# Triangular inverses of the recurrent mixer on 32x32 diagonal blocks: 48 small products in four diagonal array tiles and one eviction per step

## Chip, cores and metric

The kernel runs on one core of one Trainium2 chip (trn2). The metric is the device time of one execution in microseconds (us). Everything is float32; the large projections are made of two or three float32r passes over a high and a low part of each operand.

## What is computed

The reference is two transformer blocks over 256 tokens of width 1024. The first block's mixer has three parts, of which one is a recurrent mixer with six heads of 64 channels. This is the only part that the change touches:

```python
def step(S, inp):
    r_t, d_t, k_t, v_t, kk_t, a_t = inp
    sa = jnp.einsum('bhij,bhj->bhi', S, -kk_t)
    S = S * d_t[:, :, None, :] + sa[..., None] * (kk_t * a_t)[:, :, None, :] + v_t[..., None] * k_t[:, :, None, :]
    return S, jnp.einsum('bhij,bhj->bhi', S, r_t)

_, o = lax.scan(step, S0, tuple(tm(t) for t in (r_h, d_h, k_h, v_h, kk, a_h)))
```

The kernel does not scan token by token. It takes 32 tokens at a time: inside such a chunk the correction `sa` is the solution of a triangular system, whose matrix is unit-triangular and 32x32, so it needs the inverse (I - N)^-1 of eight chunks for each of six heads. The chunks are then joined by a state that is carried from one to the next.

## The kernel before, in words

One program for the core, written engine by engine: a block for TensorE (`pe`), VectorE (`dve`), ScalarE (`act_`), GpSimd (`pool`) and the DMA queue of SyncE. Order on each engine is the order of the code; semaphores join them. PSUM has eight banks; `opened(job)` takes the next bank in rotation and waits until its last reader gave it back, `close` signals `psum_ready`, a reader calls `take(job)` and its last instruction gives the bank back (`freed(job)`), and `copied(job)` lets TensorE wait for that.

All matmuls are issued from one helper, `mm` (line 572 before, 570 after), and transposes from lines 582 (`turn`), 1037 and others, so rows are told apart by operand names, shapes and time. A float32 product of this helper stands in the trace as two MATMUL records, each with a LDWEIGHTS record of its own; a transpose as one.

The work around the change, in the order of TensorE:

- Attention rounds of the second mixer part, with one `ada()` group after each. A group is 8 products of streamed weights (128 rows, 32 columns, 512 moving columns), in four column tiles of the array. Its weights come through a ring of six 1 MB slots.
- `gram("N", s)` and `gram("L", s)` for the two halves `s` of the tokens: 24 products of 64 rows, a 128x128 result per half and head. Heads stand as three pairs `c` with two members `p`; each (s, p) has a bank, with three 128-column results.
- VectorE multiplies those results with masks that leave 8x8 blocks of the 32x32 diagonal blocks (`U8`, `L8M`), and signals `tri_first`.
- The inverse: 11 steps, listed in `INV` (L2, N2, L4, Y1, T8, T8t, Ya, T16, T16t, Yb, T32), from 8x8 blocks by doubling to 32x32. A step is done for the four (s, p) in turn: three 128x128x128 products (or three transposes, in T8t and T16t), one bank, one eviction. Of steps that only copy, VectorE evicts p = 0 and ScalarE p = 1; of steps that add, VectorE evicts all four. The matrices are 128x128 with zeros outside the 32x32 diagonal blocks. After Y1 and after Ya stand two groups of three transposes (`tokens_out`), after T8 and T16 an `ada()` group, after Yb the gram MT of half 0.
- After T32: grams Rb and Rk of half 0, an `ada()` group, `masked_values(0)` (mv), `solved(0)` (au: the inverse times its right-hand sides, 12 products for both p in pairs of 128 columns), `blocks(0)`, and the chain over states; half 1 follows. On VectorE, after T32's evictions come six masked evictions of MT, Rb, Rk, five `low_part` of the first projection's input, and then the eviction of mv.
- The four matrices of a step lie in `TM[s][i]`, `KEEP[s][3]` holds the finished inverse. GpSimd builds the masks once, in its set-up before 31 us, ahead of the tables for the third mixer part (the S5 scan), whose last signal is `tables`.

Of the kernel before, what the change touches and what calls it, by code (L numbers as in the profile page):

```python
# [10 lines left out]
F32 = mybir.dt.float32  # L11
# [5 lines left out]
P = 128  # L17
# [56 lines left out]
def two_block_kernel(nc, a, out):  # L74
    ctx = ExitStack()
    with ctx:
# [42 lines left out]
        cond = sb("cond", KT)  # L119
        first_gain = sb("first_gain", KT)  # L120
# [33 lines left out]
        def parts(name, off, *dims):  # L154
# [54 lines left out]
        TM = [[at(M0 + 768 * i, 2, 3, P) for i in range(6)] + [at(M0 + 15360 + 768 * i, 2, 3, P) for i in range(3)],  # L209
              [at(o, 2, 3, P) for o in (2816, 3584, 4352, 5664, 6432, M0 + 17664, M0 + 18432)] +  # L210
              [place("hn_a", HN, F32, 2, 3, P), place("hn_b", HN + KT * T, F32, 2, 3, P)]]
        KEEP = [[at(M0 + 12288 + 768 * i, 2, 3, P) for i in range(4)],
                [TM[0][4], TM[0][5], TM[1][7], at(768, 2, 3, P)]]
# [271 lines left out]
        def tmat(s, i):  # L485
            return KEEP[s][3] if i == 9 else TM[s][i]

        @block.tensor
        def _(pe):
# [77 lines left out]
            def copied(job):  # L567

                pe.wait_ge(*freed(job))
# [440 lines left out]
            def gram(name, s):  # L1010
                lw, rw = {"N": (7, 6), "L": (6, 7), "MT": (8, 6), "Rb": (7, 9), "Rk": (8, 9)}[name]
# [42 lines left out]
            def solved(s):  # L1054
                copied(("mv", s))
                for p in range(2):
                    copied(("T32", s, p))
# [68 lines left out]
            for s in range(2):  # L1126
                for p in range(2):
                    copied(("N", s, p))
# [452 lines left out]
        def _(pool):  # L1581
# [44 lines left out]
            led.emit(g.tensor_tensor(L16M, L16M, L8M, ALU.subtract))  # L1626
            keep_if(row_ok[:, :], ALU.is_ge, -31, 1, [[P, 2]])
# [132 lines left out]
        def _(dve):  # L1760
# [429 lines left out]
            for s in range(2):  # L2190
                for p in range(2):
                    b = take(("N", s, p))
                    tt(TM[s][0][:, p], three(b), over3(U8), MUL, *freed(("N", s, p)))
                for p in range(2):
                    b = take(("L", s, p))
                    tt(TM[s][1][:, p], three(b), over3(L8M), MUL, sem("tri_first"))
            settle()
            for s in range(2):
                for p in range(2):
# [942 lines left out]
```

## Time and profile before

| | |
|---|---|
| three timed runs | 1310.95 us median (1309.79 to 1317.23) |
| the profiled execution | 1307.66 us, of it 1305.9 us span |
| granted TensorE clock, mean | 0.983 of 2.4 GHz |
| PE (TensorE matmul) busy | 1254.2 us, 96% of the span |
| PEld (its weight loads) busy | 1119.7 us, 86% |
| DVE (VectorE) busy | 601.3 us, 46% |
| ACT (ScalarE) busy | 653.2 us, 50% |
| POOL (GpSimd) busy | 846.8 us, 65% |
| HBM traffic | 240.11 MB read, 1.05 MB written |

Times in rows are microseconds from the span's start. "Idle before" is how long the engine stood still ahead of a row, and the arrow names what ended that. A matmul's end is modelled by the profiler, its start is recorded; busy time is the union of records, so overlapping matmuls count once, and (x96) counts records. Several records of one kind in a row are merged into one line with their count.

### The profile page before, as it was taken

The page shows a single profiled execution, that of the slowest core. Times are in us where ns is not written, and L with a number is a line of the kernel's source. Part 1 is how long each engine was busy: PE and PEld are TensorE (multiplying, and loading weights), DVE is VectorE, ACT ScalarE, POOL GpSimd, SP SyncE. Part 2 cuts the span into 40 slices and gives each one's busy share as a digit, 9 for nine tenths or more (in the row PEclk, how much of TensorE's full clock was granted, in tenths as well). Part 3 has the DMA queues.
Part 4 walks back from the last instruction along what each step waited for, and adds up shares of the span by engine and source line. Part 5 has one row for each costly group of instructions (what it writes and reads, how often), then busy time and mean ns, then how long its engine had stood idle before and what let it go on. Part 6 is the DMA issues. An engine that isn't in the chain of part 4 may idle for free.

```text
span 1305.9 us, 24860 instructions
## 1 busy us (share of the span) xinstructions
PE 1254.2 (96%) x10093; PEld 1119.7 (86%) x10093; DVE 601.3 (46%) x1369; ACT 653.2 (50%) x1074; POOL 846.8 (65%) x445
## 2 busy tenths in 40 slices
PE   6997988889999999999999999999999999999998
PEld 6993547679899999999988889998988789988887
DVE  6658687642676695432555512412111114555411
ACT  5531343125755554654666643656554554655642
POOL 8984500025788877664788777667765655888782
PEclk8998999989999999999999999999999999999999
DMA  8859895603465555435555566443648893455550
GB/s 263 214 169 376 316 343 209 212 29 102 158 194 177 171 178 186 162 129 162 161 191 183 175 194 194 130 147 113 194 134 262 266 294 120 160 189 193 178 177 33
DMA packets 232943, 242.76 MB, mean 186 GB/s; under 512 B 9196, under 2 KB 201854, under 8 KB 232830
## 3 DMA queue, kind: packets, MB, share of 16 engines
q1 hardware_dynamic: 232510, 241.08, 57.0%
q8 instruction: 80, 1.31, 0.4%
q14 instruction: 33, 0.27, 0.1%
q10 hardware_dynamic: 320, 0.10, 0.0%
HBM read 240.11 MB, written 1.05 MB: 185 GB/s over the span
## 4 chain that ended last, share of the span: by engine, by line
PE 80%; DVE 5%; ACT 2%; issue 1%; POOL 1%; DMA 0%; DVEq 0%; SPq 0%; ACTq 0%
PE banks L572 79%; DVE arena L1804 1%; DVE banks L1804 1%; DVE arena L1797 1%; PE banks L1428 1%; ACT ring_hi L2569 1%; POOL ring_lo L1716 1%; ACT arena L2569 1%; DVE hn_lo L1804 1%; DMA ring<-in_w_kv_dram 0%; DVE banks L1797 0%; DVE arena L1810 0%; PE banks L582 0%; PE banks L914 0%; PE banks L1037 0%
## 5 line engine op out<-in xcount | busy, mean ns | idle before, releaser
L1716 POOL TENSOR_TENSOR ring_lo<-ring,ring_hi 128x2048 fp32r<-128x2048 f32 (+1 forms) x176 | 717.1, 4090 | 393.4 <-ACT ring_hi L2569 392.9
L2569 ACT ACTIVATE ring_hi<-ring 128x2048 fp32r<-128x2048 f32 (+1 forms) x176 | 300.1, 1706 | 113.0 <-PE banks L572 70.2
L572 PE MATMUL banks<-hn_hi,ring_lo 128*128 128x256 f32 x1160 | 321.1, 284 | 0.0
L572 PE MATMUL banks<-hn_hi,ring_hi 128*128 128x256 f32 x992 | 279.7, 288 | 7.0 <-ACT hn_hi L2569 3.1
L2569 ACT ACTIVATE arena<-banks 128x256 f32<-128x256 f32 (+6 forms) x350 | 134.2, 399 | 275.9 <-PE banks L572 212.8
L572 PE MATMUL banks<-hn_lo,ring_hi 128*128 128x256 f32 x992 | 257.5, 284 | 0.0
L572 PEld LDWEIGHTS banks<-hn_hi,ring_lo 128*128 128x128 f32 x1160 | 221.9, 192 | 0.1
L572 PEld LDWEIGHTS banks<-hn_hi,ring_hi 128*128 128x128 f32 x992 | 191.5, 193 | 10.7 <-issue 4.4
L572 PE MATMUL banks<-hn_pair,ring_hi 128*128 128x512 f32 (+1 forms) x768 | 183.4, 374 | 0.1
L572 PEld LDWEIGHTS banks<-hn_lo,ring_hi 128*128 128x128 f32 x992 | 180.5, 193 | 0.1
L572 PEld LDWEIGHTS banks<-arena 64*32 64x32 f32 (+6 forms) x1698 | 108.8, 155 | 63.8 <-issue 39.5
L572 PE MATMUL banks<-arena 64*32 64x64 f32 (+13 forms) x1698 | 135.0, 271 | 21.4 <-DVE arena L1797 9.1
L572 PEld LDWEIGHTS banks<-hn_pair,ring_hi 128*128 128x128 f32 x768 | 135.1, 189 | 20.9 <-ACT hn_pair L2569 0.3
L1804 DVE SCALAR_TENSOR_TENSOR arena<-banks,par,arena 128x255 f32<-128x255 f32 (+1 forms) x187 | 89.6, 481 | 86.9 <-ACT arena L2569 84.4
L572 PEld LDWEIGHTS banks<-hn_pair,ring_lo 128*128 128x128 f32 x704 | 99.6, 190 | 6.2
L572 PE MATMUL banks<-hn_pair,ring_lo 128*128 128x256 f32 x704 | 104.7, 282 | 0.0
L572 PE MATMUL banks<-act_pair,ring_hi 128*128 128x512 f32 (+1 forms) x396 | 93.8, 368 | 0.0
L2569 ACT ACTIVATE arena<-banks,par 128x256 f32<-128x256 f32 x88 | 49.6, 564 | 69.6 <-DVE banks L1797 63.8
L1797 DVE TENSOR_TENSOR banks<-banks,arena 128x256 f32<-128x256 f32 x127 | 54.4, 430 | 54.7 <-ACT arena L2569 42.5
L1804 DVE SCALAR_TENSOR_TENSOR h<-banks,mod,h 128x256 f32<-128x256 f32 x46 | 22.3, 484 | 121.0 <-PE banks L572 119.7
L572 PEld LDWEIGHTS banks<-act_pair,ring_hi 128*128 128x128 f32 x396 | 68.9, 190 | 9.6
L2569 ACT ACTIVATE arena<-arena 128x256 f32<-128x256 f32 (+5 forms) x97 | 44.0, 462 | 51.1 <-DVE arena L1804 15.6
(286 smaller groups left out, 1909.5 us busy)
## 6 DMA issues: line engine op xcount, KB each, us to landing
ring<-in_ada_w_dram SPq DMA_DIRECT2D x48, 1024.0 KB, 9.1
ring<-in_ffn_w_up_dram SPq DMA_DIRECT2D x44, 1024.0 KB, 5.2
ring<-in_w_up_dram SPq DMA_DIRECT2D x22, 1024.0 KB, 5.2
ring<-in_w_kv_dram SPq DMA_DIRECT2D x34, 512.0 KB, 4.3
ring<-in_ffn_w_down_dram SPq DMA_DIRECT2D x16, 1024.0 KB, 5.3
ring<-in_w_in_dram SPq DMA_DIRECT2D x9, 1024.0 KB, 8.2
ring<-in_attn_w_q_dram SPq DMA_DIRECT2D x18, 512.0 KB, 4.0
ring<-in_kv_ada_w_dram SPq DMA_DIRECT2D x8, 1024.0 KB, 7.0
```

What stands on the lines that cost most here:

```text
L572: return nc.tensor.matmul(o, l, r, start=start, stop=stop, **k)
L1428: last = nc.tensor.transpose(b[:, k * P:k * P + P], dsc[s][:, x, k * P:k * P + P], ident[:, :])
L1716: led.emit(g.tensor_tensor(low, raw, high.bitcast(F32), ALU.subtract), sem("lo_ready"))
L1797: led.emit(v.tensor_tensor(o, x, y, op), signal, value)
L1804: led.emit(v.scalar_tensor_tensor(out=o, in0=x, scalar=s, in1=y, op0=op0, op1=op1), signal, value)
L2569: led.emit(nc.scalar.activation(o, x, func, **k), signal, value)
```

## The change

The inverse, and what feeds it, is done on the 32x32 diagonal blocks alone.

- The two token halves, two members p, three pairs c and four chunks r of a half make 48 blocks. They lie in `CHUNKS[i]`, 12 blocks of 32 columns side by side on each of the four 32-partition groups; a matrix of all 48 is 384 columns wide.
- `chunk_grams` forms N and L: 96 products of 64 rows, 32 columns, 32 moving columns, at tile positions (64p, 32r), into two banks, closed together.
- `inverse_step` makes 48 products of 32x32x32 for each step, at tile positions (32r, 32r) in rotation, into one bank, with one close. T8t and T16t are products with a 32x32 identity in place of transposes.
- One engine evicts a step, all 384 columns at once: ScalarE L2, L4, T8t and T16t (`ON_SCALAR`), VectorE the others.
- `solved` multiplies the 32x32 inverses at tile positions (32r, 32r), 24 products for each half.
- GpSimd builds `chunk_ident` in four copies and moves the masks' diagonal blocks to their first 32 columns in three.

```diff
+        CHUNKS = [at(M0 + 384 * i, 2, 6, 32) for i in range(9)] + [at(M0 + 14592, 2, 6, 32)]
...
+            def chunk_grams():
+
+                halves = [(opened(("NL", p)), slice(64 * p, 64 * p + 64)) for p in range(2)]
+                for x, (lw, rw) in enumerate(((7, 6), (6, 7))):
+                    for s in range(2):
+                        for c in range(3):
+                            o = 192 * x + 32 * (3 * s + c)
+                            for r in range(4):
+                                cut = slice(s * P + 32 * r, s * P + 32 * r + 32)
+                                for p, (b, q) in enumerate(halves):
+                                    last = mm(b[32 * r:32 * r + 32, o:o + 32], W[lw][q, c, cut], W[rw][q, c, cut],
+                                              tile_position=(64 * p, 32 * r))
+                close(last, 2)
+
             def inverse_step(name, lw, rw):
-                for s in range(2):
-                    if name == "Y1":
-                        pe.wait_ge(sem("tri_ready"), s + 1)
-                    for p in range(2):
-                        if name in ("Ya", "Yb"):
-                            pe.wait_ge(sem("tri_low"), 4)
-                        for needed in INV_NEEDS[name]:
-                            copied((needed, s, p))
-                        b = opened((name, s, p))
-                        for c in range(3):
-                            o = b[:, c * P:c * P + P]
-                            if rw is None:
-                                last = nc.tensor.transpose(o, tmat(s, lw)[:, p, c, :], ident[:, :])
-                            else:
-                                last = mm(o, tmat(s, lw)[:, p, c, :], tmat(s, rw)[:, p, c, :])
-                        close(last)
+                if name == "Y1":
+                    pe.wait_ge(sem("tri_ready"), 1)
+                if name in ("Ya", "Yb"):
+                    pe.wait_ge(sem("tri_low"), 1)
+                for needed in INV_NEEDS[name]:
+                    copied(("inv", needed))
+                b = opened(("inv", name))
+                for p in range(2):
+                    for m in range(6):
+                        o = 192 * p + 32 * m
+                        for r in range(4):
+                            q = slice(32 * r, 32 * r + 32)
+                            right = chunk_ident[q, :] if rw is None else CHUNKS[rw][q, p, m, :]
+                            last = mm(b[q, o:o + 32], CHUNKS[lw][q, p, m, :], right, tile_position=(32 * r, 32 * r))
+                close(last)
...
             def solved(s):
...
-                        last = mm(b[:, c * P:c * P + P], KEEP[s][3][:, p, c, :], AM[s][:, c, :, p * HD:p * HD + HD])
+                        for r in range(4):
+                            q = slice(32 * r, 32 * r + 32)
+                            last = mm(b[q, c * P:c * P + P], CHUNKS[9][q, p, 3 * s + c, :],
+                                      AM[s][q, c, :, p * HD:p * HD + HD], tile_position=(32 * r, 32 * r))
...
             pe.wait_ge(sem("gram_in"), 1)
-            for s in range(2):
-                gram("N", s)
-                gram("L", s)
+            chunk_grams()
             pe.wait_ge(sem("tri_first"), 4)
...
+            for r in range(4):
+                q = slice(32 * r, 32 * r + 32)
+                led.settle()
+                led.emit(g.tensor_copy(chunk_ident[q, :], ident[q, q]))
+            for r in range(1, 4):
+                q = slice(32 * r, 32 * r + 32)
+                led.settle()
+                led.emit(g.tensor_copy(masks[q, 0:4, 0:32], masks[q, 0:4, q]))
...
+            for p in range(2):
+                b = take(("NL", p))
+                tt(CHUNKS[0][:, p], shaped(b[:, 0:192], 6, 32), each(U8, 6), MUL, sem("tri_first"))
+                tt(CHUNKS[1][:, p], shaped(b[:, 192:384], 6, 32), each(L8M, 6), MUL, sem("tri_first"))
+            settle()
+            tt(both(CHUNKS[7]), both(CHUNKS[0]), each(chunk_ident, 12), ADD, sem("tri_ready"))
...
+                if name not in ON_SCALAR:
+                    b = shaped(take(("inv", name))[:, 0:384], 12, 32)
+                    if add is None:
+                        copy(both(CHUNKS[to]), b, *freed(("inv", name)))
+                    else:
+                        tt(both(CHUNKS[to]), b, both(CHUNKS[add]), ADD, *freed(("inv", name)))
                 if name == "N2":
+                    for p in range(2):
+                        dve.wait_ge(*freed(("NL", p)))
+                    tt(both(CHUNKS[2]), both(CHUNKS[3]), each(L16M, 12), MUL)
                     settle()
+                    tt(both(CHUNKS[3]), both(CHUNKS[3]), each(L32M, 12), MUL, sem("tri_low"))
```

On TensorE, from step L4 to the `ada` group after T8. Before, L4, Y1, two token transposes, T8 and the group (x counts program matmuls, each two records; "waits" names semaphores, among them the bank of each (s, p)):

```order
L572 MATMUL banks<-arena 128x128 [waits bank_free2,bank_free5,bank_free1]
L572 MATMUL banks<-arena 128x128 x2
...
L572 MATMUL banks<-arena 128x128 [waits bank_free6,bank_free1,tri_ready]
L572 MATMUL banks<-arena 128x128 x2
...
L582 MATMUL banks<-ident,arena 128x128 [waits bank_free3]
L582 MATMUL banks<-ident,arena 128x128 x2
...
L572 MATMUL banks<-arena 128x128 [waits bank_free5,bank_free6,bank_free2]
L572 MATMUL banks<-arena 128x128 x2
...
L572 MATMUL banks<-ring,late 32x512 [waits slot_landed2]
```

The same place in the changed kernel:

```order
L570 MATMUL banks<-arena 32x32 [waits bank_free4,bank_free3,bank_free2]
L570 MATMUL banks<-arena 32x32 x47
L570 MATMUL banks<-arena 32x32 [waits bank_free5,bank_free2,tri_ready]
L570 MATMUL banks<-arena 32x32 x47
L580 MATMUL banks<-ident,arena 128x128 [waits bank_free6]
L580 MATMUL banks<-ident,arena 128x128 x2
L580 MATMUL banks<-ident,arena 128x128 [waits bank_free0]
L580 MATMUL banks<-ident,arena 128x128 x2
L570 MATMUL banks<-arena 32x32 [waits bank_free1,bank_free5,bank_free4]
L570 MATMUL banks<-arena 32x32 x47
L570 MATMUL banks<-ring,late 32x512 [waits slot_landed2]
```

Each step was four pairs of rows with waits of their own and is now one wait and 48 products; its place between the other work is the same.

On VectorE, from the first masks to the masks of MT, Rb and Rk. Before:

```order
L1797 TENSOR_TENSOR arena<-banks,masks 128x384 [waits psum_ready] x8
L1797 TENSOR_TENSOR arena<-arena,ident 128x384 [waits tri_first,bank_free4,bank_free1,bank_free5,bank_free0,otok_ready]
L1797 TENSOR_TENSOR arena<-arena,ident 128x384
L1797 TENSOR_TENSOR hn_a<-arena,ident 128x384 x2
L1807 COPY arena<-banks 128x384 [waits psum_ready] x4
...
L1797 TENSOR_TENSOR arena<-banks,arena 128x384 [waits psum_ready] x4
L1797 TENSOR_TENSOR arena<-banks,masks 128x384 [waits psum_ready] x6
L1797 TENSOR_TENSOR hn_lo<-hn,hn_hi 128x256 [waits x_high] x5
L1807 COPY arena<-banks 128x3x128 [waits psum_ready]
```

And in the changed kernel:

```order
L1814 TENSOR_TENSOR arena<-banks,masks 128x192 [waits psum_ready]
L1814 TENSOR_TENSOR arena<-banks,masks 128x192
L1814 TENSOR_TENSOR arena<-banks,masks 128x192 [waits psum_ready]
L1814 TENSOR_TENSOR arena<-banks,masks 128x192
L1814 TENSOR_TENSOR arena<-arena,chunk_ident 128x384 [waits tri_first,otok_ready]
L1824 COPY arena<-banks 128x384 [waits psum_ready]
...
L1814 TENSOR_TENSOR arena<-banks,arena 128x384 [waits psum_ready]
L1814 TENSOR_TENSOR arena<-banks,masks 128x384 [waits psum_ready] x6
L1814 TENSOR_TENSOR hn_lo<-hn,hn_hi 128x256 [waits x_high] x5
L1824 COPY arena<-banks 128x3x128 [waits psum_ready]
```

The eight masked evictions of 384 columns ahead of the first step are four of 192, four evictions of a step are one, and what follows T32 stands as it did.

## Rows read from the trace of the kernel before

**Rows 1.** Busy time by stretch, whole span; x counts records, PEclk the granted clock

```profile
core 0: us, PE busy (x) PEld busy (x) DVE busy (x) ACT busy (x) POOL busy (x), PEclk, DMA share, GB/s
204.96:243.20 38.24, 36.33 (x345) 32.59 (x344) 25.05 (x49) 12.46 (x30) 0.00 (x0) 1.00 0.56 194
```

**Rows 2.** Chain of work that ended last, 205 to 245 us: start, length, what

```profile
209.81 10.98 PE banks L572 x96
220.79 0.66 PE banks L582 x6
...
225.98 1.46 PE banks L1037 x12
227.44 2.68 PE banks L572 x24
...
243.23 1.03 DVE arena L1797 x2
```

**Rows 3.** Timeline of PE, 204 to 246 us: start, length, what, idle before

```profile
204.96 2.95 PE L572 MATMUL banks<-arena 64*128 64x128 f32 x48
...
224.06 1.92 PE L572 MATMUL banks<-ring,late 128*32 128x512 f32 x16
...
244.40 1.61 PE L572 MATMUL banks<-arena 64*128 64x128 f32 x24 [1.21 <-DVE arena L1797]
...
247.79 1.55 PE L572 MATMUL banks<-arena 128*128 128x64 f32 x12
```

**Rows 4.** Timeline of DVE, 205 to 250 us

```profile
205.94 3.81 DVE L1797 TENSOR_TENSOR arena<-banks,masks 128x384 f32<-128x384 f32 x8 [2.81 <-PE banks L572]
...
245.37 1.95 DVE L1797 TENSOR_TENSOR arena<-banks,masks 128x384 f32<-128x384 f32 x4 [0.66 <-PE banks L572]
247.24 1.76 DVE L1797 TENSOR_TENSOR hn_lo<-hn,hn_hi 128x256 fp32r<-128x256 f32 x5
249.38 0.56 DVE L1807 COPY arena<-banks 128x384 f32<-128x384 f32 x1 [0.38 <-PE banks L572]
```

**Rows 5.** Timeline of PE by form at 910 us: matmuls of 64-column weights, two tiles

```profile
910.40 0.22 PE L572 MATMUL banks<-arena 128*64 128x32 f32 x1
...
910.75 0.22 PE L572 MATMUL banks<-arena 128*64 128x32 f32 x1
```

**Rows 6.** Busy time, 0.4 us of dilated attention: 32 matmuls of 64*32, 64x64, eight tiles

```profile
867.40:867.54 0.14, 0.14 (x4) 0.02 (x2) 0.00 (x0) 0.14 (x1) 0.00 (x0) 1.00 0.00 0
867.54:867.79 0.25, 0.25 (x34) 0.25 (x32) 0.00 (x0) 0.23 (x2) 0.00 (x0) 1.00 0.00 0
```

**Rows 7.** Groups by form, 89.9 to 97.4 us: the densest long run, one of its two interleaved groups

```profile
L572 PE MATMUL banks<-ring,arena 128*15 128x128 f32 x128 | 6.6, 273 | 0.0
```

**Rows 8.** Busy time by stretch around falls of the granted clock

```profile
187.60:191.00 3.40, 1.21 (x9) 1.08 (x10) 3.05 (x8) 3.21 (x7) 0.00 (x0) 1.00 1.02 379
191.00:194.40 3.40, 3.40 (x16) 1.11 (x20) 3.30 (x8) 0.60 (x1) 0.00 (x0) 0.50 0.42 160
286.60:290.00 3.40, 3.06 (x28) 2.75 (x24) 0.00 (x0) 0.30 (x1) 0.00 (x0) 1.00 0.00 0
290.00:293.40 3.40, 3.11 (x7) 2.52 (x8) 0.00 (x0) 1.14 (x4) 0.00 (x0) 0.50 0.00 0
```

**Rows 9.** Timelines of POOL and DVE: set-up copies, last table, start of the S5 scan

```profile
33.28 0.22 POOL L1662 TENSOR_TENSOR arena<-arena 128x8 f32<-128x8 f32 x1
33.58 0.20 POOL L1666 TENSOR_TENSOR arena<-arena 128x8 f32<-128x8 f32 x1
...
89.64 0.26 POOL L1674 MEMSET arena<- 128x192 f32 x1
...
90.11 2.48 DVE L1797 TENSOR_TENSOR arena<-banks,arena 128x512 f32<-128x512 f32 x4 [1.31 <-PE banks L572]
...
104.39 1.29 DVE L1797 TENSOR_TENSOR arena<-banks,arena 128x512 f32<-128x512 f32 x2 [1.59 <-PE banks L572]
```

**Rows 10.** Busy time by stretch, for the DMA columns, during the inverse

```profile
215.00:218.00 3.00, 3.00 (x29) 3.00 (x29) 2.96 (x7) 0.98 (x2) 0.00 (x0) 1.00 0.00 0
```

More of the change, by code:

```diff
@@ L119, in two_block_kernel @@
         cond = sb("cond", KT)
+        chunk_ident = sb("chunk_ident", 32)
         first_gain = sb("first_gain", KT)
@@ L208, in two_block_kernel @@
         W = [at(M0 + 768 * i, 3, T) for i in range(12)]
[L209 to L213, printed above, removed]
+        CHUNKS = [at(M0 + 384 * i, 2, 6, 32) for i in range(9)] + [at(M0 + 14592, 2, 6, 32)]
+        KEEP = [[at(M0 + 12288 + 768 * i, 2, 3, P) for i in range(3)],
+                [at(M0 + 3072, 2, 3, P), at(M0 + 3840, 2, 3, P), place("hn_a", HN, F32, 2, 3, P)]]
         tok4 = [at(M0 + 9216, 4, 3, P), at(5664, 4, 3, P)]
@@ L483, in two_block_kernel @@
                      "Ya": ("T8",), "T16": ("T8t", "Ya"), "T16t": ("T16",), "Yb": ("T16",), "T32": ("T16t", "Yb")}
-        def tmat(s, i):
-            return KEEP[s][3] if i == 9 else TM[s][i]
+        ON_SCALAR = ("L2", "L4", "T8t", "T16t")
         @block.tensor
@@ L1010, in gram @@
             def gram(name, s):
-                lw, rw = {"N": (7, 6), "L": (6, 7), "MT": (8, 6), "Rb": (7, 9), "Rk": (8, 9)}[name]
+                lw, rw = {"MT": (8, 6), "Rb": (7, 9), "Rk": (8, 9)}[name]
                 cut = slice(s * P, s * P + P)
@@ L1056, in solved @@
                 for p in range(2):
-                    copied(("T32", s, p))
+                    copied(("inv", "T32"))
                     b = opened(("au", s, p))
                     for c in range(3):
-                        last = mm(b[:, c * P:c * P + P], KEEP[s][3][:, p, c, :], AM[s][:, c, :, p * HD:p * HD + HD])
+                        for r in range(4):
+                            q = slice(32 * r, 32 * r + 32)
+                            last = mm(b[q, c * P:c * P + P], CHUNKS[9][q, p, 3 * s + c, :],
+                                      AM[s][q, c, :, p * HD:p * HD + HD], tile_position=(32 * r, 32 * r))
                     close(last)
@@ L2188, in three, with each, both @@
                 return shaped(b[:, 0:384], 3, P)
[L2190 to L2196, printed above, removed]
+            def each(m, n):
+                return m[:, 0:32].unsqueeze(1).broadcast_to([P, n, 32])
+            def both(x):
+                return x.rearrange("p a b c -> p (a b) c")
+            for p in range(2):
+                b = take(("NL", p))
+                tt(CHUNKS[0][:, p], shaped(b[:, 0:192], 6, 32), each(U8, 6), MUL, sem("tri_first"))
+                tt(CHUNKS[1][:, p], shaped(b[:, 192:384], 6, 32), each(L8M, 6), MUL, sem("tri_first"))
             settle()
-            for s in range(2):
-                for p in range(2):
-                    tt(TM[s][7][:, p], TM[s][0][:, p], over3(ident[:, :]), ADD, sem("tri_ready") if p else None)
+            tt(both(CHUNKS[7]), both(CHUNKS[0]), each(chunk_ident, 12), ADD, sem("tri_ready"))
             def masked(names, s):
@@ L2595, in reach @@
                     if n < 2:
-                        act_.wait_ge(*freed(("T32", 1, 0)))
-                        act_.wait_ge(*freed(("T32", 1, 1)))
+                        act_.wait_ge(*freed(("inv", "T32")))
                     for x in before:
@@ L2800, in _ @@
                 high_part(hn_hi[:, 6 + m, :], hn[:, 6 + m, :])
-            for s in range(2):
-                for p in range(2):
-                    act_.wait_ge(sem("tri_first"), 2 * s + p + 1)
-                    b = take(("L", s, p))
-                    af(TM[s][3][:, p], shaped(b[:, 0:384], 3, P), ACT.Identity, *freed(("L", s, p)))
+            for p in range(2):
+                act_.wait_ge(sem("tri_first"), 2 * p + 2)
+                b = take(("NL", p))
+                af(CHUNKS[3][:, p], shaped(b[:, 192:384], 6, 32), ACT.Identity, *freed(("NL", p)))
             def tokens_out(s, xs):
@@ L2815, in _ @@
             for name, _l, _r, add, dst_ in INV:
-                if add is None:
-                    for s in range(2):
-                        b = take((name, s, 1))
-                        af(tmat(s, dst_)[:, 1], shaped(b[:, 0:384], 3, P), ACT.Identity, *freed((name, s, 1)))
+                if name in ON_SCALAR:
+                    b = take(("inv", name))
+                    af(CHUNKS[dst_].rearrange("p a b c -> p (a b c)"), b[:, 0:384], ACT.Identity, *freed(("inv", name)))
                 if name in ("Y1", "Ya"):
```

17 lines of the change are left out of this document (removed).

## The prediction, made blind

> **What bounds the kernel now.** I read the page first: TensorE is busy for 96% of the span, so the question is what the 38 us of the inverse do there. The busy time by stretch [rows 1] shows 36.3 of 38.2 us busy, at the full granted clock, with no GpSimd work and VectorE at 25 us: while the inverse runs, TensorE sets the time. The chain of waits [rows 2] says the same: from 209.81 on it is matmuls without a break, and VectorE appears in it only after T32, for 1.03 us. The PE timeline [rows 3] gives the grams of N and L (2.95 us), the `ada` group (1.92 us), and one real wait, 1.21 us ahead of gram Rb. The DVE timeline [rows 4] gives the eight first masks, 3.81 us. The grams close half by half, so those masks begin at 205.94 under them; from the grams' end at 207.91 TensorE stands for 1.90 us.
>
> **What a product costs.** A 128x128x128 product is two matmul records: 24 records take 2.68 us [rows 2], 112 ns each, and a step is 12 products. Two transposing steps take 1.46 us each.
>
> The changed step has 96 records of 32 columns in four tiles. No row has that shape, so I take it from its neighbours. A tile that holds 128-column weights takes a new record every 112 ns; with 64-column weights, two tiles side by side, the records of one tile start 58 ns apart: from 910.40 to 910.75 are six of them [rows 5]. The line through the two gives 31 ns for 32 columns, so four tiles give 7.8 ns for each record, if they really run side by side. Eight tiles do: 32 matmuls begin within 0.25 us [rows 6], also 7.8 ns each. So a step is 96 x 7.8 = 0.75 us. It is a choice: the run in rows 6 is 32 records long, and a step has 96. The longest dense run in this trace is the compressed-key product, 256 records in two interleaved groups of 128 over 6.6 us and a little more [rows 7], 27 ns each. It has 128 moving columns, so the array alone explains it, but nothing longer is faster. Bounds of a record are therefore 7.8 and 27 ns; I take 7.8 because rows 5 and 6 are nearer in shape and no row shows supply running short.
>
> **The sum, removed work.**
> - Steps: nine product steps of 2.68 and two of 1.46 are 27.0 us. Eleven of 0.75 are 8.3. **-18.8 us**.
> - Grams N and L: 48 records in 2.95 us become 192, in eight tiles, at 7.8 ns: 1.5, and 0.2 for the last one's length [rows 5]. **-1.2 us**.
> - Masks ahead of L2: eight of 0.48 us become four of half the width, between 0.24 and 0.48 us; I take 0.29, 1.15 in all, now wholly exposed because the two banks close together. TensorE's stand goes from 1.90 to 1.25. **-0.65 us**.
> - `solved`: 12 records of 112 ns for each half become 48, of 128 moving columns in four tiles, 28 ns each: 1.34 either way. **0**.
> - After T32, four evictions on VectorE are one, so gram Rb no longer finds VectorE behind: **-1.2 us** [rows 3].
>
> **Added work and waits.**
> - A step whose result the next one needs at once now stands bare: 0.22 us for the last matmul [rows 5], 0.56 for the eviction [rows 4], 0.1 for two semaphores, 0.88 us. N2 before L4 has nothing between: 0.9. Y1 before T8, and Ya before T16, have 0.66 us of token transposes between [rows 2]: 0.2 each. Yb before T32 has gram MT, 12 records at half of Rb and Rk's 1.61 [rows 3], 0.8: 0.1. T8 and T16 are followed by `ada`, 1.92 us, which covers them; the evictions of L2, L4, T8t and T16t run under the next step. **+1.4 us**.
> - Behind N2's eviction on VectorE stand two masks of 384 columns (L16M, L32M, 0.5 us each) and then Y1's eviction; Y1 ends 1.7 us after L4 begins, so they fit.
> - The array changes its tile shape about eight times more. In rows 6 weight loads pause for 0.12 of 0.14 us at such a place. **+0.8 us**.
> - VectorE after T32: 0.56 for T32, six masks of 0.49 and five `low_part` in 1.76 [rows 4] are 5.3 us, then mv's eviction. TensorE needs 1.6 for Rb and Rk, 1.92 for `ada`, 1.55 for mv, 5.1. `blocks(0)` is late by **+0.3 us** where it was covered.
>
> That is -19.4 us at full clock. Two terms more:
>
> - **Clock.** Where TensorE did little for some us, the granted clock then stood at 0.50 of 2.4 GHz, that is 1.2 GHz: after 1.21 us busy in 3.4 [rows 8], but also after 3.06 us busy with matmuls of few columns. Now L2 to Y1 use a quarter of the array, with waits between. I expect one or two stretches of 3.4 us at 1.2 GHz, in which half the work gets done: 1.7 to 3.4 us, **+2.5**. Ends: 0, and all of the stage at 1.2 GHz (below).
> - **GpSimd's set-up.** Seven small copies, each behind a wait; such pairs start 0.30 us apart [rows 9], so `tables` comes 2.1 us later than 89.90. The S5 scan needs it; VectorE has 0.2 us to spare before its start at 90.11, and 1.59 at 104.39, where it waits for TensorE. **+0.3** (0 to 2.1).
>
> **Net -16.6 us.** On the profiled execution: 1307.66 - 16.6 = 1291.1. The timed median of before is 3.3 us above the profiled one, so against it: 1310.95 - 16.6 = **1294.4 us**.
>
> **What could eat it later.** The `ada` weights are not late: DMA stands at 0 GB/s at 215 to 218 [rows 10], since all ring slots are full, and each further group is asked for only as its slot falls free. After 290 TensorE is the bound, and GpSimd's first conversions hang on events of this stage, so they move with it. I cost both at nothing.
>
> **Rivals.**
> - *Supply runs short after the burst.* If LDWEIGHTS and MATMUL come to the array at some 16 ns a pair (twice the burst rate; an estimate between 7.8 and 27), the 11 steps cost 8.7 us more and the grams 1.6, less about 1.0 of clock: gain 7.3 us, **1303.6**. For it: no run beyond 32 records. Against it: in rows 6 the loads keep up.
> - *A floor near 25 ns a record.* 1056 + 192 = 1248 records x 17.2 ns = 21.5 us, against 19.4: 2 us slower than before without the clock's term, about **1313**. Rows 6 speak against it: 32 records start in 0.25 us. The Trainium skill, "TensorE: Matmul & The Clock Gate", section "Wait — 56ns, not 53.3ns?", says that start-to-start never drops below about 25 ns however small the moving side; by that rule the sum is this one and not mine. The trace disagrees with it over eight tiles, for 32 records.
> - *The four diagonal tiles do not run side by side (the other side).* Then each record takes the 31 ns of one tile: 1248 x 23.2 = 29 us more, less 19.4, **+9.6 us, 1320.5**. It decides from 7.8 + 19.4/1248 x 1000 = 23 ns a record on; above 28.6 it is slower by over 0.5%. For it: rows 6 show tiles of two row groups, none on the diagonal. Against: nothing in rows 5 and 6 serializes tiles.
> - *The whole stage at 1.2 GHz.* Steps 8.3, grams 1.5, transposes 1.3, MT, Rb, Rk 2.4 and two `ada` 3.8 double: +17 us in place of 2.5, less the waits that they then cover, 2: gain 4, **1307**. For it: 3.06 us busy did not hold the clock at 286.6 [rows 8]. Against: `ada`, Rb and Rk fill the array between.
>
> **Chances.** Forecast 0.65; supply short 0.15; floor 0.07; no overlap 0.05; cold stage 0.08. Forecast range: clock 0 to 5, set-up 0 to 2.1, masks and shape changes 1 either way: 1289 to 1300. The range given, **1289 to 1307**, takes in short supply and the cold stage, and leaves out the floor, no overlap and a rest. 0.5% is 6.6 us, about what a measurement of this kernel can tell from no change. Faster: 0.65, 0.09 of short supply (its 7.3 is near the bound) and 0.02 of the cold stage, 0.76. Same: 0.06, 0.06 and the floor's 0.07, 0.19. Slower: 0.05.
>
> **What would show it.** Right: 32x32 groups of 96 records about 0.95 us long with the last one's length, VectorE or ScalarE as releaser ahead of L4 alone for about 0.9 us, T32's end near 224 and not 243, gram Rb without a wait, clock 0.50 for at most two stretches there. Wrong: groups of 1.5 us and more (supply), 2.4 (floor), 3 (no overlap); a wait on a ring slot ahead of `ada`; the S5 scan beginning 2 us late and everything after it too; a gain at 290 that is gone at the end.

## The result, and the profile after it

The changed kernel takes 1318.91 us (median of 13 runs, 1315.49 to 1328.72), the kernel before, beside it, 1311.05 us (13 runs, 1308.02 to 1320.7). The ratio is 1.0055, with an interval of 1.0029 to 1.0081: slower by about 7 us, where I had forecast 16.6 us less. The time lies outside the range that I gave.

| | before | after |
|---|---|---|
| span of the profiled execution | 1305.9 us | 1316.4 us |
| mean granted clock of TensorE | 0.983 | 0.970 |
| first gram to mv's product | 204.96 to 247.79 | 207.63 to 258.69 |
| that stretch | 42.83 us | 51.06 us |
| from there to the end | 1058.1 us | 1057.7 us |
| MATMUL records in the trace | 10093 | 11125 |

The stretch from the first record of the grams to the first of mv's product is the measure in all that follows. It accounts for 8.2 us of the 10.5 between the two spans. Another 2.7 lie ahead of the grams. I hold them for scatter: of two profiled executions of one and the same kernel (e3 and e7 below) one begins its grams at 207.96 and the other at 210.61. Behind the stretch 0.4 us is won.

Busy time by stretch, first the kernel before and then the changed one (columns: the stretch, its length, busy time and instructions of PE, PEld, DVE, ACT and POOL, granted clock, DMA share, GB/s):

```profile
204.96:247.79 42.83, 39.72 (x385) 34.45 (x385) 28.95 (x58) 12.46 (x30) 0.00 (x0) 1.00 0.50 173
```

```profile
207.63:258.69 51.06, 31.43 (x1345) 22.93 (x1344) 10.50 (x23) 6.50 (x18) 0.00 (x0) 0.70 0.43 147
```

TensorE is busy for 8 us less and idle for 19.6 us where it was idle for 3.1; and the mean clock is 0.70. The waits of TensorE in this stretch of the changed kernel (us in total, times, longest):

```profile
PE banks L570 <- issue: 18.4, 10, 4.2
PE banks L570 <- DVE arena L1814: 1.2, 1, 1.2
```

The profile names no releaser for 18.4 us of it: "issue" is time in which an engine waited for nothing that the profile shows. The timeline of PE shows where (a row that merges several shapes bears the shape of its first record):

```profile
207.63 1.39 PE L570 MATMUL banks<-arena 64*32 64x32 f32 x141
212.62 0.73 PE L570 MATMUL banks<-arena 64*32 64x32 f32 x51 [3.59 <-issue]
214.59 1.28 PE L570 MATMUL banks<-arena 32*32 32x32 f32 x76 [1.25 <-DVE arena L1814]
218.09 1.81 PE L570 MATMUL banks<-arena 32*32 32x32 f32 x116 [2.22 <-issue]
220.60 0.42 PE L570 MATMUL banks<-arena 32*32 32x32 f32 x12 [0.69 <-issue]
221.66 1.92 PE L570 MATMUL banks<-arena 32*32 32x32 f32 x127 [0.63 <-issue]
225.24 0.96 PE L570 MATMUL banks<-arena 32*32 32x32 f32 x53 [1.67 <-issue]
...
231.49 0.92 PE L570 MATMUL banks<-chunk_ident,arena 32*32 32x32 f32 x84
233.02 0.31 PE L570 MATMUL banks<-chunk_ident,arena 32*32 32x32 f32 x12 [0.62 <-issue]
233.19 1.01 PE L570 MATMUL banks<-arena 32*32 32x32 f32 x96
234.13 0.88 PE L580 MATMUL banks<-ident,arena 128*128 128x128 f32 x6
234.94 0.31 PE L570 MATMUL banks<-arena 32*32 32x32 f32 x13
239.40 1.02 PE L570 MATMUL banks<-arena 32*32 32x32 f32 x83 [4.15 <-issue]
240.35 3.42 PE L570 MATMUL banks<-ring,late 128*32 128x512 f32 x16
...
249.47 3.54 PE L570 MATMUL banks<-arena 32*32 32x32 f32 x127 [4.18 <-issue]
```

Count the records between two pauses. From 212.62: 51 + 76 = 127. From 218.09: 116 + 12 = 128. From 221.66: 127. The pauses break off in the midst of a group, not between steps, and they come each 127 or 128 records whatever the step. Each record has its own LDWEIGHTS, so that is 256 instructions. Only from 239.40 on are there 255 records (83, 16, 96 and 60) without a pause between; an `ada` group of 3.42 us stands in their first half. One wait among the ten is of another kind: 0.69 us at 220.60 is L4 waiting for N2's eviction. The other nine are 17.7 us.

The trace also holds the DMA packets, by queue. Queue q8 carries TensorE's instructions, in packets of 16 KB: the trace of the changed kernel has 88 of them for 22687 instruction records of TensorE (matmuls, weight loads, semaphores), 258 for each. The pause from 235.25 to 239.40, seen from 235 on in 40 slices (DMA is the busy share of the engines in tenths):

```profile
DMA  9999999999999999999998997630101000010000
...
q8 instruction: 1, 0.02, 1.6%
```

One instruction packet of 16 KB runs in this window, from 236.81 to 237.91, and the DMA engines are full of weights up to about 237.7. TensorE starts again at 239.40, 1.5 us after the packet has landed. At the other pauses of this stretch that delay is 1.2 to 1.5 us. So the reading from the trace is: **TensorE had no instructions left.** Before the change a block of 256 instructions lasted 10 to 14 us here, with records of a step 112 ns apart, and no wait of this stretch is put down to "issue".

The granted clock fell in three places of the stretch, for 31 us in all; in the kernel before it was 1.00 throughout. They are all lines but that of 229.80:

```profile
212.60:229.80 17.20, 10.51 (x541) 9.24 (x545) 3.99 (x10) 2.62 (x6) 0.00 (x0) 0.50 0.21 74
229.80:240.00 10.20, 5.43 (x296) 3.56 (x292) 0.98 (x2) 1.36 (x3) 0.00 (x0) 1.00 0.58 209
240.00:243.40 3.40, 3.40 (x52) 0.88 (x38) 0.56 (x1) 0.00 (x0) 0.00 (x0) 0.50 0.06 6
246.80:257.00 10.20, 7.11 (x172) 6.26 (x175) 3.29 (x7) 0.00 (x0) 0.00 (x0) 0.50 0.33 107
```

A clock of 0.50 is 1.2 GHz, 1.00 is 2.4. An `ada` group of 16 records takes 3.42 us there (240.35) against 1.92 at full clock [rows 3].

### The profile page after: what moved, and what is told of

Read it like the earlier page. It is cut to its first block, busy times and chain, and to the rows that moved or that the text cites. A ratio compares the mean times of both kernels' runs of the same rounds, so it can differ in the third digit from the quotient of the medians.

```text
span 1316.4 us, 26845 instructions
## 1 busy us (share of the span) xinstructions
PE 1251.1 (95%) x11125; PEld 1111.2 (84%) x11125; DVE 577.6 (44%) x1333; ACT 646.5 (49%) x1062; POOL 848.5 (64%) x452
## 4 chain that ended last, share of the span: by engine, by line
PE 73%; DVE 3%; ACT 1%; POOL 1%; issue 1%; DVEq 0%; ACTq 0%
PE banks L570 72%; POOL ring_lo L1733 1%; DVE banks L1821 1%; PE banks L1437 1%; ACT ring_hi L2583 1%; DVE arena L1821 1%; DVE hn_lo L1821 1%; DVE banks L1814 0%; DVE arena L1814 0%; ACT hn_hi L2583 0%; ACT arena L2583 0%; DVE h L1821 0%; ACT banks L2583 0%; PE banks L1223 0%; PE banks L580 0%
## 5 line engine op out<-in xcount | busy, mean ns | idle before, releaser
L2583 ACT ACTIVATE arena<-banks 128x256 f32<-128x256 f32 (+7 forms) x339 | 128.6, 394 | 294.6 <-PE banks L570 233.7
L570 PEld LDWEIGHTS banks<-hn_hi,ring_hi 128*128 128x128 f32 x992 | 191.4, 193 | 10.5 <-ACT hn_hi L2583 4.4
L570 PEld LDWEIGHTS banks<-arena 32*32 32x32 f32 (+6 forms) x2562 | 101.6, 144 | 81.0 <-issue 57.1
L570 PE MATMUL banks<-arena 32*32 32x32 f32 (+13 forms) x2562 | 129.4, 254 | 37.1 <-issue 22.1
```

Source lines behind the costliest of these rows:

```text
L570: return nc.tensor.matmul(o, l, r, start=start, stop=stop, **k)
L2583: led.emit(nc.scalar.activation(o, x, func, **k), signal, value)
```

## The experiments

The theory to be tested is that the supply of instructions sets the pace of the changed stretch. Its rivals are the array and its clock, and small tiles as such.

### The disputed cost by itself (e6_burst_before)

The kernel before, unchanged but for a burst of small products on constants ahead of T8, where the DMA engines stand:

```diff
                         b = opened((name, s, p))
+                        for m in range(192 if (name, s, p) == ("T8", 0, 0) else 0):
+                            q = slice(32 * (m % 4), 32 * (m % 4) + 32)
+                            mm(b[q, 32 * (m % 12):32 * (m % 12) + 32], ident[q, q], ident[q, q],
+                               tile_position=(32 * (m % 4), 32 * (m % 4)))
                         for c in range(3):
```

> The kernel before, with 192 more 32x32 products (384 records, 768 instructions, on constants, into a bank that T8 then fills) ahead of T8's first group, where the DMA engines stand and the clock is full: the disputed cost by itself. My prediction's price: 384 x 7.8 ns = 3.0 us. Theory (supply): one block of 256 instructions may already be there, the next two or three take 3.6 to 4 us each without DMA traffic: 8 to 11 us, in runs of 128 records at 7.8 ns with pauses of 2.5 us between, each ended 1.3 to 1.5 us after a packet of instructions. A floor of 25 ns a record with no pauses: 9.6 us, even starts; so the trace decides between the last two, not the sum.

The burst took 10.19 us (227.98 to 238.17), the whole kernel 1325.98 us against 1311.72 beside it (ratio 1.0107, 1.0058 to 1.0156). The timeline of PE by form:

```profile
227.98 1.14 PE L572 MATMUL banks<-ident 32*32 32x32 f32 x111
230.89 1.27 PE L572 MATMUL banks<-ident 32*32 32x32 f32 x128 [1.78 <-issue]
234.35 1.93 PE L572 MATMUL banks<-ident 32*32 32x32 f32 x128 [2.18 <-issue]
237.80 0.44 PE L572 MATMUL banks<-ident 32*32 32x32 f32 x17 [1.53 <-issue]
```

This separates my price, an even floor of 25 ns and a supply in blocks. Within a run the records start as fast as I had predicted: 128 take 1.27 us and 111 take 1.14, so 17 more cost 0.13 us, 7.6 ns each. So there is no floor of 25 ns within a run. The rule that I quoted from the Trainium skill, "TensorE: Matmul & The Clock Gate", section "Wait — 56ns, not 53.3ns?", is contradicted here over 128 records. But a block of 128 records begins each 3.46 us (230.89, 234.35) and 3.45 us (237.80), the first with its records at full clock, the second at 1.2 GHz. The pace doesn't depend on the clock of the array: a run that takes longer is followed by a shorter pause. So, with no other DMA traffic, **256 instructions cost 3.45 us: 13.5 ns an instruction, 27 ns a product record.** (Two blocks of e2 below took 3.36 us.) The DMA view of this stretch, 228 to 238 us in 40 slices, shows that the only traffic is three instruction packets:

```profile
DMA  0020000000000000200000000000020000000000
...
q8 instruction: 3, 0.05, 1.9%
```

The trace's packet records divide the 3.45 us. The second and third packet start 1.2 and 1.0 us after the first record of the block before (230.89, 234.35), a packet takes 1.0 to 1.1 us, and TensorE starts again 1.2 to 1.4 us after it has landed. One block is brought at a time: ahead of the burst no packet of q8 moves from 214.14 to 228.68, though the DMA engines are idle from about 220 on, and in the kernel before one packet comes for each 256 instructions, however long they last. Where weights are loaded, it is the start of the packet that is late and not its transfer: in the changed kernel it comes 1.0 to 1.6 us after a block's first record where no load runs or one is ending, and 2.7 to 3.8 us after it where loads fill the DMA engines (212.61, 233.02 and 243.94), while a transfer takes 0.9 to 1.4 us everywhere.

The whole kernel lost 14 us by the medians where the burst took 10; the interval (8 to 20 us) holds both.

The Trainium skill, "Runtime: NRT & Kernel Launch", section "Instruction fetch mechanics", says that the sequencer fetches its stream itself in blocks of 16 KiB, 256 instructions, and that crossing a block is mostly hidden. The block size agrees with the 128 records of two instructions each; hidden it is here only where a block's work lasts longer than 3.45 us, and beside weight loads longer than that.

### Twice the small grams (e4_grams_twice)

```diff
-                for x, (lw, rw) in enumerate(((7, 6), (6, 7))):
+                for x, (lw, rw) in 2 * tuple(enumerate(((7, 6), (6, 7)))):
```

> The changed kernel, with the 192 records of the small grams of N and L issued twice (same outputs). Theory (supply): 384 more instructions are 1.5 blocks of 256 of 3.6 to 5.5 us, so +5 to +8 us in the stretch and in the total. Rival (my sum's price of a record, 7.8 ns): +1.5 us, or +3 us at 1.2 GHz.

Measured: 1327.63 us against 1313.44 for before (ratio 1.0115, 1.0086 to 1.0144); by the two ratios that is some 8 us above the changed kernel. The stretch took 55.68 us in place of 51.06, 4.6 more: a little under what supply foretold, three times my price, and half as much again as that price at 1.2 GHz. TensorE is idle for 2.0 us more and busy for 2.7 more, at a mean clock of 0.66, so this run alone would not part supply from clock. The pauses here, beside the weight loads, are longer than in the burst above:

```profile
211.73 1.39 PE L570 MATMUL banks<-arena 64*32 64x32 f32 x141
216.18 1.28 PE L570 MATMUL banks<-arena 64*32 64x32 f32 x128 [3.06 <-issue]
222.10 1.44 PE L570 MATMUL banks<-arena 64*32 64x32 f32 x115 [4.64 <-issue]
```

From 216.18 to 222.10 one block of 256 instructions takes 5.9 us.

### Weight loads held back (e2_loads_held)

In SyncE's queue, for the loads into the slots that the `ada` groups behind T8 and T16 set free (`held_groups` has their numbers):

```diff
                     sp.wait_ge(*chunk_used[order[n - SLOTS]])
+                    if order[n - SLOTS][0] == "ada" and order[n - SLOTS][1] in held_groups:
+                        sp.wait_ge(*freed(("inv", "T32")))
```

> The changed kernel, with the weight loads that the ada groups behind T8 and T16 set free held until T32's eviction, so that the DMA engines carry nothing but instructions from about 216 us to T32. Theory (instruction packets wait behind weight loads): the two pauses of 4.2 and 4.4 us behind such loads become about 2 us each, every block of 256 instructions takes 3.6 to 4.0 us, and T32 comes 4 to 6 us earlier against the grams; what the later loads lose may give 1 to 3 us of it back, total 2 to 5 us faster than the changed kernel. Rival (the pauses have nothing to do with DMA traffic, but with TensorE's own queue or clock): T32 in its place within 1 us, total the same or slower by the later loads.

Measured: 1315.99 us against 1313.44 (ratio 1.0021, 0.9996 to 1.0047), stretch 46.39 us in place of 51.06. The two long pauses, of 4.15 and 4.18 us, became:

```profile
236.73 0.91 PE L572 MATMUL banks<-arena 32*32 32x32 f32 x83 [1.13 <-issue]
...
243.66 3.54 PE L572 MATMUL banks<-arena 32*32 32x32 f32 x127 [2.23 <-issue]
```

Together that is 5.0 us less, about the whole of the 4.7 us by which the stretch is shorter; it lies within the 4 to 6 that I expected. Instructions come by the same DMA engines as the weights, and a packet asked for while a load runs comes late. In the total I can't tell the gain for sure: the intervals of the two ratios overlap, and the held loads have to be made up later. In the profiled execution the part behind the stretch took 1065.8 us in place of 1057.7.

### One tile after another (e1_tile_by_tile)

The same 96 records a step, in an order in which no two tiles can overlap:

```diff
-                for p in range(2):
-                    for m in range(6):
-                        o = 192 * p + 32 * m
-                        for r in range(4):
-                            q = slice(32 * r, 32 * r + 32)
+                for r in range(4):
+                    q = slice(32 * r, 32 * r + 32)
+                    for p in range(2):
+                        for m in range(6):
+                            o = 192 * p + 32 * m
```

> The changed kernel, with the 96 records of a step in another order: all 24 of one diagonal tile, then all of the next, so that no two tiles work side by side. Theory (the supply of instructions): in the changed kernel TensorE stands 0.5 to 4.4 us after each 127 or 128 records, that is each 256 instructions, and starts again 1.3 to 1.5 us after a 16-KB instruction packet has landed; one such block takes 3.6 us at the least, whatever is in it. A step tile by tile is then 96 x 31 ns = 3.0 us of array, 128 records 4.0 us, which lies nearly wholly in that time: the stretch from the grams to T32 grows by 0 to 8 us, not by the 25 us that the array alone would add, and the pauses shrink. Rival (the array and its clock set the time; at 1.2 GHz a record of one tile is 62 ns): 11 steps x 2.2 us = +25 us at least.

Measured: 1339.24 us against 1313.44 (ratio 1.0207, 1.0182 to 1.0232), stretch 72.89 us, 21.8 more than the changed kernel's. My expectation from the supply, 0 to 8 us, was wrong, and the rival's 25 us was nearly right: I had counted the array at full clock. It stood at 1.2 GHz for nearly all of it:

```profile
213.00:260.70 47.70, 46.51 (x812) 39.63 (x810) 4.28 (x8) 3.60 (x8) 0.00 (x0) 0.50 0.17 60
```

The longest run is 192 records in one piece, without a pause:

```profile
223.29 9.11 PE L570 MATMUL banks<-arena 32*32 32x32 f32 x192 [0.70 <-issue]
```

47 ns a record, so 128 of them take 6.1 us, more than a block's 3.45, and the pauses fell from ten of 18.4 us in sum to four of 4.6 us. These are the instructions of the changed kernel in another order, so it is not small tiles as such that make the pauses: a block costs the larger of the two, its work and its fetch. With the work made long, as here, the array and its clock set the time. And the four diagonal tiles do work side by side in the changed kernel. TensorE was busy here, 46.5 of 47.7 us, for the most part with one tile of 32x32 at a time, and the clock was at its lower level all the same.

### Blocks of 64x64 (e3_blocks_64, e7_blocks_64_again)

If 27 ns a record is the supply's price at its best, the tile to take is the one whose records take the array about as long. [Rows 5] had that: two tiles with 64 columns start a record every 29 ns. So the change's own idea with 64x64 blocks, half as many products (the layout, and the heart of `inverse_step`):

```diff
-        CHUNKS = [at(M0 + 384 * i, 2, 6, 32) for i in range(9)] + [at(M0 + 14592, 2, 6, 32)]
+        CHUNKS = [at(M0 + 768 * i, 2, 6, 64) for i in range(6)] + [at(M0 + 15360 + 768 * i, 2, 6, 64) for i in range(3)] + \
+            [at(M0 + 14592, 2, 6, 64)]
...
                 for p in range(2):
+                    if name == "Y1":
+                        pe.wait_ge(sem("tri_ready"), p + 1)
+                    for needed in INV_NEEDS[name]:
+                        copied(("inv", needed, p))
+                    b = opened(("inv", name, p))
                     for m in range(6):
-                        o = 192 * p + 32 * m
-                        for r in range(4):
-                            q = slice(32 * r, 32 * r + 32)
+                        for r in range(2):
+                            q = slice(64 * r, 64 * r + 64)
                             right = chunk_ident[q, :] if rw is None else CHUNKS[rw][q, p, m, :]
-                            last = mm(b[q, o:o + 32], CHUNKS[lw][q, p, m, :], right, tile_position=(32 * r, 32 * r))
-                close(last)
+                            last = mm(b[q, 64 * m:64 * m + 64], CHUNKS[lw][q, p, m, :], right,
+                                      tile_position=(64 * r, 64 * r))
+                    close(last)
```

Grams, `solved`, masks and evictions follow; evictions are by halves p again, of 384 columns each.

> The change's idea on 64x64 diagonal blocks: two diagonal tiles, 24 products or 48 records a step (half of the changed kernel's, twice the kernel before's), evictions by halves again. By the array a record of one such tile is 58 ns, two side by side 29 ns, a step 1.4 us against 2.68 before. Theory (supply of 256 instructions in 3.6 us and more, 28 ns a record): supply and array are level, few pauses, grams to T32 28 to 32 us against 38 before and 46 changed; total 1299 to 1304, 7 to 12 us faster than before. Rival (small tiles as such are what costs: clock at 1.2 GHz or tile switches): the stretch takes as long as the changed kernel's 46 us or at the least as before's 38.

Measured: 1306.4 us against 1313.44 for before (ratio 0.9938, 0.9914 to 0.9963), stretch 32.25 us, 10.6 below before and 18.8 below the changed kernel. To gram Rb it was 29.5 us, within the 28 to 32 that I had expected to T32; the total came out 2 us above the expected range, against a before that was itself 2 us higher in these runs.

```profile
207.96:240.21 32.25, 28.70 (x721) 22.65 (x720) 16.36 (x33) 8.14 (x21) 0.00 (x0) 1.00 0.66 232
```

The granted clock is 1.00, though the products of the steps fill only half of the array. A step is 48 records in 1.6 us, 33 ns each, and one pause is left, behind the weight loads at 208 to 216 us:

```profile
207.96 1.63 PE L569 MATMUL banks<-arena 64*64 64x64 f32 x96
210.97 5.51 PE L569 MATMUL banks<-arena 64*64 64x64 f32 x169 [1.38 <-DVE arena L1812]
218.31 0.91 PE L569 MATMUL banks<-arena 64*64 64x64 f32 x23 [1.83 <-issue]
219.16 0.87 PE L579 MATMUL banks<-ident,arena 128*128 128x128 f32 x6
219.96 1.61 PE L569 MATMUL banks<-arena 64*64 64x64 f32 x48
```

Once more, beside another set of runs:

> The kernel with 64x64 blocks once more, beside e5 on the same chip: 0.5 to 0.8% faster than before again, 1304 to 1307 us.

1301.46 us against 1311.72 (ratio 0.9932, 0.9909 to 0.9954), stretch 33.14 us. This version is faster than both kernels, by 0.6 to 0.7% than the one before.

### Two attempts on the pause that is left (e5_blocks_64_held, e8_tokens_first)

In e5 the loads into slots freed by the last two `ada` groups ahead of the grams wait for the end of N2:

```diff
+                    if order[n - SLOTS][0] == "ada" and order[n - SLOTS][1] in held_groups:
+                        sp.wait_ge(psum_ready, job_no[("inv", "N2", 1)] + 1)
```

> The kernel with 64x64 blocks (e3), with the weight loads that the last two ada groups before the grams set free held until N2 has ended, so that they don't run at 208 to 216 us beside the first instruction packets of the stage. Theory (packets wait behind weight loads): the one pause left in e3, 1.8 us at 216.5 to 218.3, shrinks below 0.5 us or goes, the grams to Rb take 27.5 to 28.5 us in place of 29.5; total 1 to 2 us below e3, if the later ada groups find their weights landed. Rival (pause not from DMA traffic): the pause stays, or the held loads come late and T16's ada waits: total same as e3 or 1 to 3 us slower.

1303.76 us against 1311.72 (ratio 0.9939, 0.9911 to 0.9967), stretch 32.31 us: the same as e3. The pause went (192 records from 210.00 on without one), and two others came, in the `ada` group behind T16 and in Yb, where the held loads now ran; an instruction packet landed 1.4 us ahead of each restart:

```profile
227.53 1.06 PE L571 MATMUL banks<-ring,late 128*32 128x512 f32 x7 [0.59 <-issue]
...
234.06 2.19 PE L571 MATMUL banks<-arena 64*64 64x64 f32 x50 [1.16 <-issue]
```

In e8 the token transposes move to behind the grams, under VectorE's masks:

```diff
             chunk_grams()
+            tokens_out(0, range(4))
...
-                if name == "Y1":
-                    tokens_out(0, (0, 1))
-                elif name == "Ya":
-                    tokens_out(0, (2, 3))
-                elif name == "Yb":
+                if name == "Yb":
```

> The kernel with 64x64 blocks (e3), with the four token transposes of s=0 (24 records, 1.75 us) moved from behind Y1 and Ya to right behind the grams, where TensorE stands 1.6 us for VectorE's masks. By halves a step of 64x64 blocks runs 1.5 us, so the half that the next step needs first is evicted under the other half, and the transposes are no longer needed as a cover. Expected: no idle time of TensorE between the grams and L2, 0.0 to 0.3 us new ahead of T8 and T16; but the first blocks of instructions are used up sooner, while the weight loads run, so the pause of 1.8 us may grow by part of it. Grams to mv's product 30.9 to 32 us in place of 32.25; total 0 to 1.4 us below e3, which the median can't show. Rival (supply sets this place): the pause grows by the whole 1.6 us, and nothing is gained.

1303.58 us against 1311.54 (ratio 0.9937, 0.9915 to 0.9959), stretch 33.27 us against 32.25 and 33.14 in the two runs of the 64x64 kernel. The 1.4 us of waiting for the masks went, as meant (0.3 left for VectorE in the whole stretch), and the pauses for instructions grew from 2.2 us (e7) to 3.9. The rival that I wrote down holds here, in the one profiled execution: where supply is level with the array, a wait taken away comes back at the next block.

## Why the prediction was wrong

**The step that failed** is the price of a record over a long run: "I take 7.8 because rows 5 and 6 are nearer in shape and no row shows supply running short". That the shape is nearer was right. The price was read from a run of 32 records [rows 6], a quarter of a block of 256 instructions, too short to show anything of the supply. Measured, a record costs 7.6 ns within a run at full clock, but a block of 128 cost 3.56 us and more in the changed kernel, and up to 6.38 beside weight loads, where my price makes 1.0 us. That put 17.7 us of pauses into the stretch, which the sum had at nothing.

The row that priced it was in my hands: the compressed keys, 256 records [rows 7], 27 ns each. (The 6.6 us of that row are the busy time of one of two interleaved groups; the 256 records start from 89.99 to 97.00, in 7.0 us.) I wrote that "the array alone explains it". It does, and the supply explains it as well; in that run the two are level, so it can't speak for either. A bound that two mechanisms explain stays a bound for both.

A pause put down to "issue" is no proof of short supply by itself. The kernel before has one of 1.43 us at 88.91:

```profile
88.91 1.15 PE L572 MATMUL banks<-arena 32*128 32x256 f32 x12 [1.43 <-issue]
```

It stands between two groups, no packet of q8 lands from 73.24 until 91.63, and TensorE starts again 0.1 us after VectorE's work of 87.69 to 88.81 has ended; the changed kernel has the same wait, of 1.43 us, at 89.60. So it is more likely a wait for VectorE. What marks the pauses of the inverse is the packet that lands 1.2 to 1.5 us ahead of the restart.

**The rivals.** I had "supply runs short after the burst" at 16 ns a pair with a chance of 0.15, as a slower stream. It is a stream in blocks, at some 27 ns a record at its best and up to 50 (6.38 us for 128 records) beside weight loads. With 27 ns for all 1248 records my own sum gives "a floor near 25 ns" over again, about 1313 us, and 2.5 more for 27 in place of 25; how the rest up to 1318.9 divides between the loads and the clock is not measured. The loss of 7.9 us lies between those of my second rival (2) and my third (9.6), and the mechanism was nearest to that of my first. By my own reckoning, which turns "from 7.8 + 19.4/1248 x 1000 = 23 ns a record on", the change could only lose.

**Term by term**, with the stretch forecast at 42.8 - 19.6 + 2.5 = 25.7 us and measured at 51.1 (19.6 are the prediction's 19.4 without the 0.3 of `blocks(0)`, which lies behind the stretch):

- Groups of 96 records "about 0.95 us long": 1.01 at 233.19. Right, and with it that the four diagonal tiles run side by side. One tile's record, 31 ns by the line through rows 5, starts each 31.7 ns in e1 at full clock (from 260.93 on).
- Masks and TensorE's stand ahead of L2, 1.15 and 1.25 us: both as predicted.

```profile
213.39 1.15 DVE L1814 TENSOR_TENSOR arena<-banks,masks 128x192 f32<-128x192 f32 x4 [7.57 <-PE banks L570]
```

- L4's wait for N2, 0.9 us: 0.93 from the last start ahead of it to its own (220.60). Right; no other step wait stands in the list beside the pauses.
- Gram Rb without a wait: right, none is in the list of waits.
- `solved`, 0: 1.51 us against 1.60. Right.
- GpSimd's set-up, +0.3: no cost found. `tables` came 1.3 us later (91.21 for 89.90), not 2.1, and VectorE waits for TensorE, not for GpSimd, ahead of the S5 scan; it begins 1.4 us later than in [rows 9] with all the work ahead of it.

```profile
91.53 2.48 DVE L1814 TENSOR_TENSOR arena<-banks,arena 128x512 f32<-128x512 f32 x4 [2.04 <-PE banks L570]
```

- Clock, +2.5: 31 us of the stretch stood at 1.2 GHz, not 3.4 or 6.8. Of the 25.4 us between forecast and measurement the pauses are 17.7 and what is left, 7.7, I put down to this; it is argued and not shown by a run of its own. An estimate from the rows above says that it can be most of it: in the three places at 0.50 TensorE was busy for 10.51 + 3.40 + 7.11 = 21.0 us; at full clock that work would take half at the least, so the clock cost at most 10.5 us, of which the forecast has 2.5. (An `ada` group takes 3.42 us in place of 1.92, 128 small records take 1.93 in place of 1.27, so it is less than 10.5.) The kernel with 64x64 blocks had none of it in this stretch, so it came with the pauses or with the 32x32 tiles, not with small products in general; in e1, with one 32x32 tile at a time, it fell behind a pause too (3.07 us at 210.97), but then stayed down from 217.0 to 260.7 with no pause longer than 0.7 us. The rival "the whole stage at 1.2 GHz" was right on the clock for three fifths of the stretch, and wrong that this would be the main loss.
- "What could eat it later": `ada` weights were not late, as I said. I had looked only at whether the loads come in time, not at what they hold up: the instruction packets.

## What to carry to other kernels

Count instructions, not only columns: in these runs TensorE got 256 instructions in about 3.4 us at best and in up to 6.4 beside weight loads, so a stretch whose matmul and weight-load pairs start closer than about 27 ns, for longer than a block, is bound by its instruction stream, and more and smaller products there only add instructions. The sign in a profile is "<-issue" in the midst of a group, each 128 records, with an instruction packet landing shortly before the restart. When making tiles smaller, stop at the size whose records take the array as long as the stream takes to bring them: here two 64x64 tiles (33 ns a record in e3), which gave 10 us of the stretch where four of 32x32 lost 8.

## What I had not expected of the hardware

- Slow work ahead of the burst in e6 had not built up a stock of instructions: TensorE had just run 96 records of 128x128 products, for 12 us, and yet the first pause came after 111 small ones. No packet had come for 14.5 us, and the next one, from 228.68 to 229.64, started only under the burst: nothing beyond the block in use was there.
- Instruction packets share the DMA engines with the weights, and start late beside them: pauses of 4.15 and 4.18 us beside loads, 1.13 and 2.23 without.
- 46.5 us busy of 47.7, mostly one 32x32 tile at a time (e1), did not bring TensorE back to its upper clock level; 28.7 busy of 32.3, mostly on two 64x64 tiles (e3), kept it there.
- What stays open: why the clock fell in the changed kernel, by the pauses or by its tiles, and what holds a packet back beside weight loads. In e5 and e8 the pauses moved rather than shrank, and no run takes the weight loads away altogether.
